# Modulation sums of a two-block model: from one matmul column per half unit to pairs in four groups of 32 output rows, turned once per batch

## What is computed

```python
c_act = jax.nn.silu(c)
for l in range(DEPTH):                      # first block, DEPTH = 2
    ada = c_act @ w_ada[l] + b_ada[l]       # 1024 x 3072
    shift, scale, gate = jnp.split(ada, 3, axis=-1)
    h = rmsnorm(x, norm_g[l]) * (1.0 + scale[:, None, :]) + shift[:, None, :]
    p = h @ w_in[l]
    ...                                     # 4 mLSTM heads, 4 retention heads
    x = x + gate[:, None, :] * (y @ w_out[l])
...
for l in range(DEPTH):                      # second block: six parts, 1024 x 6144
    h = modulate(rmsnorm_2(x, norm_mix_g[l]), sh1, sc1)
    ...                                     # convolution and banded attention
    x = x + g1[:, None, :] * y
    h = modulate(rmsnorm_2(x, norm_ffn_g[l]), sh2, sc2)
    f = swiglu(h, ...) if l % 2 == 0 else moe_swiglu(h, ...)
    x = x + g2[:, None, :] * f
```

## Time and profile before

| what | value |
|---|---|
| median of 3 runs | 2113.82 us (2112.89 to 2114.36) |
| span of the profiled execution | 2109.6 us |
| PE busy | 2063.4 us, 98% |
| DVE busy | 1759.2 us, 83% |
| ACT busy | 1321.1 us, 63% |
| beside heads and out units, layer 1 / layer 2 | about 60 to 340 / 345 to 640 us |
| feed-forward, gate and up / down | about 767 to 900 / 900 to 967 us |

### The profile page before, as it was taken

How to read it: one execution, slowest core, us unless ns; L and a number is a source line. 1 busy time by engine, 2 the same in 40 slices (tenths; PEclk the granted TensorE clock), 3 DMA queues, 4 the chain that set the end, 5 groups by cost and what they waited for, 6 DMA issues and landing times.

```text
span 2109.6 us, 33770 instructions
## 1 busy us (share of the span) xinstructions
PE 2063.4 (98%) x13553; PEld 1837.5 (87%) x13553; DVE 1759.2 (83%) x2177; ACT 1321.1 (63%) x1265; POOL 30.5 (1%) x60
## 2 busy tenths in 40 slices
PE   7999999999999999999989999999999999999998
PEld 5999999999999889999878888888888888888887
DVE  3898976888759888888878888888888888888887
ACT  3655645566645663435757777776777776776775
POOL 3000000000000000000000000000000000000000
PEclk8999999999999999999999999999999999999999
DMA  9788855776656379986448999999999999999995
GB/s 297 248 261 249 250 199 160 220 220 204 216 184 220 117 225 308 317 308 220 141 163 306 361 355 348 379 348 347 357 356 376 349 345 356 365 365 344 360 344 195
DMA packets 356160, 595.05 MB, mean 282 GB/s; under 512 B 10376, under 2 KB 201368, under 8 KB 356008
## 3 DMA queue, kind: packets, MB, share of 16 engines
q1 hardware_dynamic: 352864, 586.92, 80.7%
q0 software_dynamic: 2752, 5.86, 1.1%
q10 hardware_dynamic: 392, 0.13, 0.0%
HBM read 591.80 MB, written 4.22 MB: 283 GB/s over the span
## 4 chain that ended last, share of the span: by engine, by line
PE 84%; DVE 9%; ACT 3%; issue 2%; DMA 1%; POOL 0%; SPq 0%; DVEq 0%; POOLq 0%
PE ps L1660 9%; PE ps L1662 9%; PE ps L1661 9%; PE ps L1150 6%; PE ps L1152 5%; PE ps L1151 5%; PE ps L1691 5%; PE ps L1690 5%; PE ps L1689 5%; PE ps L1205 3%; PE ps L1207 3%; PE ps L1206 3%; DVE wlo L1757 3%; PE ps L1635 1%; PE ps L1478 1%
## 5 line engine op out<-in xcount | busy, mean ns | idle before, releaser
L1757 DVE TENSOR_TENSOR wlo<-raw,whi 128x2048 fp32r<-128x2048 f32 x485 | 1108.9, 2288 | 206.9 <-ACT whi L730 206.5
L730 ACT CAST whi<-raw 128x2048 fp32r<-128x2048 f32 x485 | 926.6, 1911 | 376.2 <-PE ps L1662 133.2
L1150 PE MATMUL ps<-hhi,whi 128*128 128x256 f32 x1360 | 387.4, 285 | 0.5 <-DVE wlo L1757 0.5
L1152 PE MATMUL ps<-hhi,wlo 128*128 128x256 f32 x1360 | 379.8, 279 | 0.0
L1151 PE MATMUL ps<-hlo,whi 128*128 128x256 f32 x1360 | 379.5, 279 | 0.0
L1660 PE MATMUL ps<-whi,xghi 128*128 128x512 f32 x896 | 360.3, 402 | 0.7 <-DVE wlo L1757 0.7
L1662 PE MATMUL ps<-wlo,xghi 128*128 128x512 f32 x896 | 350.2, 391 | 0.0
L1661 PE MATMUL ps<-whi,xglo 128*128 128x512 f32 x896 | 348.9, 389 | 0.0
L1150 PEld LDWEIGHTS ps<-hhi,whi 128*128 128x128 f32 x1360 | 255.8, 188 | 7.6 <-issue 7.3
L1151 PEld LDWEIGHTS ps<-hlo,whi 128*128 128x128 f32 x1360 | 255.9, 188 | 0.3
L1152 PEld LDWEIGHTS ps<-hhi,wlo 128*128 128x128 f32 x1360 | 255.6, 188 | 0.0
(11 more groups left out here) (400 smaller groups left out, 2991.4 us busy)
## 6 DMA issues: line engine op xcount, KB each, us to landing
raw<-in_moe_w_gate_dram SPq DMA_DIRECT2D x112, 1024.0 KB, 5.9
raw<-in_moe_w_up_dram SPq DMA_DIRECT2D x112, 1024.0 KB, 5.8
raw<-in_moe_w_down_dram SPq DMA_DIRECT2D x112, 1024.0 KB, 5.2
raw<-in_w_in_dram SPq DMA_DIRECT2D x92, 1024.0 KB, 5.5
raw<-in_w_ada_dram SPq DMA_DIRECT2D x69, 1024.0 KB, 7.9
raw<-in_w_out_dram SPq DMA_DIRECT2D x24, 1024.0 KB, 5.2
raw<-in_ffn_w_gate_dram SPq DMA_DIRECT2D x11, 1024.0 KB, 9.2
raw<-in_ffn_w_up_dram SPq DMA_DIRECT2D x11, 1024.0 KB, 9.1
```

The lines of the kernel that those rows point to most:

```text
L730: nc.scalar.copy(whi[:, u.hl, :], raw[:, u.raw, :]).then_inc(hi_ready, 1)
L1150: mm(ps2[u.bank][:, j], whi[:, u.hl, w], hhi[:, k], start=k == 0, stop=False)
L1152: last = mm(ps2[u.bank][:, j], wlo[:, u.hl, w], hhi[:, k], start=False, stop=k == KD - 1)
L1757: V.tensor_tensor(wlo[:, u.hl, :], raw[:, u.raw, :], whi[:, u.hl, :].bitcast(F32), ALU.subtract).then_inc(raw_free, 1)
```

## The change

`ada` becomes `ada_pair`. The operands change places: now `acc` is streamed (128 columns) and `onepad` is held, a band of 32 columns, zero but for a column of ones. With the band shifted by r, the sums fall into row r of a group of 32 PSUM partitions. The four halves of two units go to the four groups, r counts the pairs of a batch, and the matmuls of a batch add up in the same 128 x 128 area `summed`. When a batch is whole, ACT copies it (`take_sums`), PE turns it by the identity (`turn_sums`), and DVE takes all from the turned area in the order of rows and groups. A batch is a turn of two heads (9 or 6 units) or the feed-forward part (24 units). The places change with it: PE adds up at the second unit of a pair; `ADA_FF_AT` places the last three modulation units at steps 27, 28 and 29 instead of 28, 29 and 30; and DVE's `take_pair` moves behind the third weight unit of head 2, or behind the fourth out unit.

```diff
-ADA_SUMMED = (((7, 9, 10, 11, 12, 15, 16, 17, 17), (4, 6, 7, 8, 10, 11, 15, 16, 17)),
-              ((6, 9, 11, 12, 15, 17), (4, 6, 8, 12, 15, 17)))
+ADA_SUMMED = (((8, 10, 14, 16, 17), (5, 8, 11, 15, 17)),
+              ((8, 11, 17), (5, 11, 17)))
+ADA_FF_AT = tuple(j for j in range(27) if j % 4 != 3) + (27, 28, 29)
...
 def ada_beside_ff(j):
-    return j - j // 4 if j >= 0 and j % 4 != 3 and j - j // 4 < ADA_FF else None
+    return ADA_FF_AT.index(j) if j in ADA_FF_AT else None
...
+        onepad = sb("onepad", [P, 2 * GROUP - 1])
...
+        summed, summed_turned = ps[7][:, S:S + P], ps[7][:, S + P:S + 2 * P]
...
+            def take_sums(to, last):
+                act.wait_ge(ext_out, 16)
+                act.wait_ge(ada_done, last.count())
+                nc.scalar.copy(to, summed).then_inc(row_copied, 1)
...
-            def ada(a, bank):
-
-                pe.wait_ge(ada_free, a.sums())
-                for j in range(2):
-                    last = mm(bank[:, a.col + j:a.col + j + 1], acc[:, a.n % HALF, j * P:(j + 1) * P], ones[:, 0:1],
-                              start=True, stop=True)
-                last.then_inc(ada_done, 1)
+            def ada_pair(units, r):
+                of = units[2 * r:2 * r + 2]
+                for i, (a, *_) in enumerate(of):
+                    pe.wait_ge(ada_free, a.sums())
+                    for j in range(2):
+                        g = GROUP * (2 * i + j)
+                        last = mm(summed[g:g + GROUP], onepad[:, GROUP - 1 - r:2 * GROUP - 1 - r], acc[:, a.n % HALF, j * P:(j + 1) * P],
+                                  start=r == 0, stop=2 * (r + 1) >= len(units), skip_group_check=True)
+                    last.then_inc(ada_done, 1)
+
+            def turn_sums(of, copied):
+                pe.wait_ge(row_copied, copied)
+                nc.tensor.transpose(summed_turned, of, ident).then_inc(mod_turned, 1)
...
             for j in range(DOWN_UNITS):
                 pe.wait_ge(flo_ready, j + 1)
                 rows_product(Unit(S_FF + FF_UNITS + j), fhi, flo, 2 * j, j == 0, j == DOWN_UNITS - 1)
-                if ada_beside_ff(FF_UNITS + j - 1) is not None:
-                    ada(ADA_AT_FF[ada_beside_ff(FF_UNITS + j - 1)][0], ps[7])
+                i = ada_beside_ff(FF_UNITS + j - 1)
+                if i is not None and i % 2:
+                    ada_pair(ADA_AT_FF, i // 2)
+                if j == DOWN_UNITS - 2:
+                    turn_sums(sumsf[:], 9)
```

More of the change, by code:

```diff
@@ L173, in __init__ @@
     def __init__(self, n, first):
-        self.n, self.col = n, 2 * (n - first)
+        self.n, self.first = n, first
     def count(self, k=1):
@@ L327, in two_block_model @@
         acol = sb("acol", [P, 2, H], F32, b1)
-        relx = sb("relx", [L * NH2, EXT], F32, b1)
+        relx_or_sums = sb("relx_or_sums", [P, EXT], F32, b1)
+        relx, sums1 = relx_or_sums[0:L * NH2], relx_or_sums[:, 0:P]
         b1.close()
@@ L390, in two_block_model @@
         fa = sb("fa", [P, 2, 2, S], F32, bf)
+        sumsf = sb("sumsf", [P, P], F32, bf)
         bf.close()
@@ L847, in _ @@
                     high(q.plus(LOOK))
+                    if h_no == 2:
+                        take_sums(sums1, (ada_l0, ada_l1)[l](0)[-1][0])
                     act.wait_ge(unit_done, q.done())
@@ L905, in _ @@
                     high(Unit(S_B1 + l * UNIT_L1 + H * HEAD_UNITS + j + LOOK))
+                    if j == 0:
+                        take_sums(sums1, (ada_l0, ada_l1)[l](1)[-1][0])
                     if j < 3:
@@ L1056, in _ @@
                 high(Unit(S_FF + FF_UNITS + j + LOOK))
+                if j == DOWN_UNITS - 2:
+                    take_sums(sumsf[:], ADA_AT_FF[-1][0])
             mixer(1, S_B3)
@@ L1348, in _ @@
                     ada_after(1)
+                    if h_no == 2:
+                        turn_sums(sums1, 2 * l + 5)
                     if h_no:
@@ L1413, in _ @@
                     rows_product(Unit(S_B1 + l * UNIT_L1 + H * HEAD_UNITS + j), yhi, ylo, 2 * j, j == 0, j == OUT1_UNITS - 1)
+                    if j == 1:
+                        turn_sums(sums1, 2 * l + 6)
                     if j < 2:
@@ L1573, in _ @@
                     products(Unit(S_FF + j))
-                if ada_beside_ff(j - 1) is not None:
-                    ada(ADA_AT_FF[ada_beside_ff(j - 1)][0], ps[7])
+                i = ada_beside_ff(j - 1)
+                if i is not None and i % 2:
+                    ada_pair(ADA_AT_FF, i // 2)
             for j in range(DOWN_UNITS):
@@ L1816, in ada, with take_mod @@
                 V.tensor_tensor(sums[0], sums[0], sums[1], ALU.add).then_inc(ada_free, 1)
-            def take_mod(bank, col, n, block, l, at):
+            def take_mod(r, n, block, l, at):
                 par, base = (par1, P1_BADA) if block == 0 else (par2, P2_BADA)
-                to = 3 * KD * (3 * l + block)
-                return V.tensor_tensor(mod[:, bass.ds(at * 2 + to, 2 * n)], bank[:, col:col + 2 * n],
-                                       par[:, l, bass.ds(at * 2 + base, 2 * n)], ALU.add)
+                to, of = 3 * KD * (3 * l + block) + 2 * at, base + 2 * at
+                g = min(2 * n, 4)
+                return V.tensor_tensor(mod[:, to:to + 2 * n].rearrange("p (r g) -> p r g", g=g),
+                                       summed_turned.rearrange("p (g r) -> p r g", g=4)[:, r:r + 2 * n // g, 0:g],
+                                       par[:, l, of:of + 2 * n].rearrange("p (r g) -> p r g", g=g), ALU.add)
             def amuls(norms):
@@ L1831, in amuls @@
                 step(last)
+            step(V.memset(onepad[:], 0.0))
+            V.memset(onepad[:, GROUP - 1:GROUP], 1.0)
             step(V.memset(ones[:], 1.0))
@@ L1959, in take_pair @@
                 ada_units = (ada_l0, ada_l1)[l](pair)
-                dve.wait_ge(ada_done, ada_units[-1][0].count())
+                dve.wait_ge(mod_turned, 5 + 2 * l + pair)
                 if l == 0:
-                    take_mod(ps[7], 0, 2, *ada_units[0][1:])
-                    take_mod(ps[7], 4, 6, *ada_units[2][1:])
-                    take_mod(ps[7], 16, 1, *ada_units[8][1:]).then_inc(mod_taken, 1)
+                    take_mod(0, 2, *ada_units[0][1:])
+                    take_mod(1, 6, *ada_units[2][1:])
+                    take_mod(4, 1, *ada_units[8][1:]).then_inc(mod_taken, 1)
                 else:
-                    take_mod(ps[7], 0, ADA_TURN[1], *ada_units[0][1:]).then_inc(mod_taken, 1)
+                    take_mod(0, ADA_TURN[1], *ada_units[0][1:]).then_inc(mod_taken, 1)
             def angles():
@@ L2006, in _ @@
                     low(q.plus(LOOK))
-                    if h_no == 2:
-                        take_pair(l, 0)
                     ada_after(0)
@@ L2036, in _ @@
                     low(v.plus(LOOK))
+                    if h_no == 2:
+                        take_pair(l, 0)
                     if h_no:
@@ L2088, in _ @@
                     if j == 0:
+                        add_squares(Head(l, H - 1), 1)
+                    if j == 3:
                         take_pair(l, 1)
-                    if j == 0:
-                        add_squares(Head(l, H - 1), 1)
                     if j == 2:
@@ L2310, in _ @@
                     ff_low(FF_UNITS // 2 - 1)
-            dve.wait_ge(ada_done, A_MIX1)
-            take_mod(ps[7], 0, 4, *ADA_AT_FF[0][1:])
-            take_mod(ps[7], 8, ADA_FF - 4, *ADA_AT_FF[4][1:]).then_inc(mod_taken, 1)
+            dve.wait_ge(mod_turned, 9)
+            take_mod(0, 4, *ADA_AT_FF[0][1:])
+            take_mod(2, ADA_FF - 4, *ADA_AT_FF[4][1:]).then_inc(mod_taken, 1)
             dve.wait_ge(mod_taken, 6)
```

3 lines of the change are left out of this document (2 added, 1 removed).

## The result

| what | before | after |
|---|---|---|
| median, runs on one chip | 2113.66 us (2111.32 to 2115.08, 6 runs) | 2120.55 us (2116.33 to 2122.1, 6 runs) |
| ratio of the times | | 1.003, 95% interval 1.0019 to 1.004 |
| span of the profiled execution | 2109.6 us | 2118.9 us |
| forecast | | 2118.9 us, 2112.5 to 2122.5 |

The changed kernel takes 6.9 us more by the medians and 9.3 us more by the two profiled executions. D0 to D10 are the down units.

What follows compares the result with a forecast made beforehand. PE is busy 98%, but DVE sets its pace in places. First layer -1.55, second +1.1, gate and up +0.1 (already within the next), down units -4.65: 5.1 us slower, 2113.8 + 5.1 = 2118.9 us; range 2112.5 to 2122.5.

Steps and rivals of the forecast that it cites:

- Rival 1: Down units: no stall, the load lands in time or DVE makes it up; 2113.2 us, no change; chance 0.2.
- rival 2: Whole kernel: PE's 98% binds, DVE comes forward with it, neither stall occurs; 6.5 us less, 2107.3 us; chance 0.06.
- rival 4: First layer, head 1: only the head's stall is missing; 2116.9 us, inside no change; chance 0.12.
- rival 3: Pairs on PE: the column groups don't overlap, 1.0 us a pair, 6 us more in all, 2125 us; chance 0.12.
- signs that would have made it wrong: Stage from 760 to 900 us shorter, casts in the down stage no later than before, or a pair over 0.8 us.
- Cost of a pair: On PE, summing two modulation units together: 0.57 us, bounds 0.45 and 1.0, against 0.44 for each old insertion.
- Cost of a turn: On PE, five new turns: 0.3 us each with the slow first product, 1.5 us together.
- First layer: Heads and out stage: 1.55 us lost, of which 2.0 from PE waiting 3.3 us for unit 7's sum in head 1.
- Second layer: Heads and out stage: sums ready 3 us or more before PE comes, so cheaper pairs gain 1.1 us.
- Gate and up: Feed-forward: PE saves 2.5 to 3 us on paper, but DVE's round sets the pace; gain taken as 0.1 us.
- Down units: Feed-forward: D6's weight load held behind a modulation load, PE then waits 3.2 and 2.7 us; 4.65 us lost.

Runs made afterwards that it cites:

- e4: The changed kernel with its new steps, but the last three modulation loads again sent behind the next weight load, as before: 2112.88 us, 0.9995 of the kernel before.
- e10: The changed kernel with 24 unused matmuls ahead of each of the three pairs for which PE waits: 2120.56 us, 1.0025 of the kernel before.
- e8: The kernel before, with half of each modulation sum beside the feed-forward part left out on DVE: 2111.09 us, 0.9987 of the kernel before.
- e9: The changed kernel, with half of each modulation sum beside the feed-forward part left out on DVE: 2104.51 us, 0.9958 of the kernel before.
- e1: The changed kernel with the last three feed-forward modulation units, and their loads, back at steps 28, 29 and 30: 2111.86 us, 0.9985 of the kernel before.
- e6: The kernel before, with only the last three feed-forward modulation units and their loads moved one step earlier: 2123.55 us, 1.0049 of the kernel before.
- e5: The changed kernel with only the modulation load ahead of D6's weights put back behind them: 2116.36 us, 1.0006 of the kernel before.

## Why the prediction was right

**Direction, size, range.** Slower was forecast as the likeliest, 2118.9 us; 2120.55 came. Rival 1 (no stall in the down units) falls by the rows of D6 and by e4, rival 2 (the gain comes through) and rival 4 by the head's stall, rival 3 by the 0.55 us of a pair. Of the signs that would have made it wrong none came: gate and up didn't get shorter, D6's cast was late, and a pair takes less than 0.8 us.

**Cost of a pair: right.** 0.57 forecast, 0.55 measured where nothing is waited for. The entry is the 0.09 of the earlier trace rows. The eight records take 0.35, where two rounds and the start of the groups were put at 0.26. The way out takes 0.11 with the slow first gap, where 0.17 was put, and the 0.05 for the wait inside the pair isn't there: the terms' errors cancel. The Trainium skill says in "TensorEngine Tiling (Array Packing)", Key Properties, that a change of the tiling mode drains the engine. The 0.09 us going in agrees with it, as the old form had no such gap; of the 0.11 coming out the old form, which switches nothing, had 0.08 already. The wait between the two units does split the eight records, but only where it really waits: then they come as four and four, as at 161.27 and 164.42. That much of rival 3 is true, but there PE is waiting anyway.

**Cost of a turn: too high.** 0.3 us was taken, from f32 matmuls with two records. A turn leaves one record and costs 0.11. Five turns cost 0.55 us, not 1.5.

**First layer: the place and the wait right, the size low.** 1.55 forecast, 2.93 measured. The sum ended at 164.36 (forecast 164.29). The net loss at the next head was 3.45, not 2.0. The term that failed is the step from the end of the pair to the next head. It took every product at full speed, and the ninth product ran partly at 1.2 GHz. e10 measures that: at 2.4 GHz the loss is 1.74. Behind the stall 0.5 us came back, 0.45 forecast.

**Second layer: near.** A gain of 1.1 was forecast and 3.1 seen, of which 1.6 is a slow stretch that the changed kernel's trace lacks; 1.5 is left.

**Gate and up: right, and the reason holds.** A gain of 0.1 forecast, a loss of 0.15 measured; e8 and e9 show the 3.0 us that PE alone would gain ("on paper 2.5 to 3", though from 17 insertions where the trace has 16). What the text had too sharp is that DVE's round alone binds: with half the sums gone the old kernel gained 2.8 us there, 1.55 of it at the first sum, and then PE binds.

**Down units: the mechanism right step by step, the size low.** D6's cast was put at 931.3 and came at 931.97; the sum at 938.9 and 939.56 (DVE waited 4.37 us for the cast, about 4 was put); D7's start at 945.3 and 945.52; then the second wait. D10 was put at 966.15 and came at 968.34. Two terms make the 2.2 us. The load behind the late sum was used at 947.40, not 946.3, so D9 started at 960.96 instead of 960.1, 0.9 us. And from D9 to D10 it took 7.38 us instead of 6.05: D9 ran into 1.2 GHz, which cost 1.5 us (5.89 in e10), while the turn cost 0.2 less than forecast. e1, e4 and e6 show that it is the place of the loads and that nothing else in the change is needed for it.

**What was luck.** By D10 the account is +6.8 and the forecast was 5.1, but the terms were further off than that: 1.4 too little in the first layer, 2.2 in the down units, and 2.0 too little gain in the second layer, 1.6 of it a slow stretch that before happened to have. The forecast left the clock out altogether, and it is in each of the three. That its errors of opposite sign leave 1.7 us at D10, and the median within 1.7 us of the forecast, is luck in part.

## What to carry to other kernels

Before you cheapen an instruction of the busiest engine, look where it stands: at each place where a second engine delivers within a few tenths of a microsecond, the gain stops, and it is had only when both are relieved (e9). When several small steps are grouped, the group comes at the time of its last member, so put it behind the step at which that member is ready. And a table of steps moves loads too: a load that waits for a slot, placed ahead of others in an ordered queue, holds all of them, and here that cost more than the new form could bring.

## What the runs showed of the hardware that I had not expected

- Behind two of the three waits of 2.5 to 2.7 us TensorE's granted clock fell to 1.2 GHz (0.61 and 0.66 in the windows), which cost 1.5 to 1.7 us more than the wait. Behind the third, at D7, just as long (2.50 us), D7's products ran at full speed; in e5 that same place had the slow stretch. At the end of head 1 it came in six traces of six with the long wait, and in two of three with the old wait of about 1 us. Filled with unused matmuls, the three places stayed at 2.4 GHz, and the total didn't change.
- The router's work ran at a mean granted clock of 0.51 in the changed kernel (1102.03 to 1118.47) and 0.88 before (1095.35 to 1109.05), 2.7 us apart. It isn't the change: in e8, the kernel before with half sums, the windows 1095 to 1107 are at 0.50 too. Two single profiles of this kernel can't settle 3 us.
- A transpose of a 128 x 128 f32 tile leaves one record and takes 0.11 us in a row of matmuls, where an f32 matmul of 128 columns leaves two records and takes about 0.18 us.
